# Expert down pieces of a two-layer decoder trunk: the output bank becomes the outermost loop

## The reference

```python
def swiglu(h, w_gate, w_up, w_down):
    return (jax.nn.silu(h @ w_gate) * (h @ w_up)) @ w_down

def moe_swiglu(h, w_router, w_gate, w_up, w_down):
    ...
    for e in range(N_EXPERTS):
        out = out + comb[..., e:e + 1].astype(h.dtype) * swiglu(h, w_gate[e], w_up[e], w_down[e])
    return out
```

## Time and profile before

| what | value |
|---|---|
| median of 3 runs | 1414.81 us (1414.27 to 1415.77) |
| the profiled execution's own time | 1414.73 us |
| its span, first to last instruction | 1412.9 us |
| TensorE busy with matmuls | 1391.1 us, 10414 matmuls |
| VectorE busy / ScalarE busy | 1141.0 us / 920.1 us |
| HBM over the span | 312 GB/s |
| mean granted TensorE clock | 0.997 of full speed |
| stretch of the experts' matmuls | about 445 us to 1400 us |

### The profile page before, as it was taken

How to read it: one execution, slowest core, us unless ns; L and a number is a source line. 1 busy time by engine, 2 the same in 40 slices (tenths; PEclk the granted TensorE clock), 3 DMA queues, 4 the chain that set the end, 5 groups by cost and what they waited for, 6 DMA issues and landing times.

```text
span 1412.9 us, 24835 instructions
## 1 busy us (share of the span) xinstructions
PE 1391.1 (98%) x10414; PEld 1263.2 (89%) x10416; DVE 1141.0 (81%) x1042; ACT 920.1 (65%) x901; POOL 61.1 (4%) x72
## 2 busy tenths in 40 slices
PE   9999999999999999999999999999999999999996
PEld 7899999998888988888888888888888888888884
DVE  6676555558756999888988888888898898888886
ACT  3845444444445777777777777777777777777764
POOL 2030000003001200000000000000000000000030
PEclk9999999999999999999999999999999999999998
DMA  8456765554217999999999999999999999999951
GB/s 344 149 209 231 249 230 187 202 184 145 96 55 314 419 407 415 379 393 366 377 378 393 372 377 393 367 379 387 361 382 377 398 367 379 390 375 370 376 200 47
DMA packets 63582, 438.64 MB, mean 310 GB/s; under 512 B 7550, under 2 KB 7678, under 8 KB 12272
## 3 DMA queue, kind: packets, MB, share of 16 engines
q1 hardware_dynamic: 58752, 422.60, 78.5%
q10 hardware_dynamic: 3568, 10.57, 2.2%
q0 software_dynamic: 1152, 3.88, 0.8%
HBM read 431.44 MB, written 9.04 MB: 312 GB/s over the span
## 4 chain that ended last, share of the span: by engine, by line
PE 96%; POOL 2%; DVE 1%; ACT 1%; issue 0%; DMA 0%; DVEq 0%; POOLq 0%; ACTq 0%
PE ps L1909 43%; PE ps L1934 22%; PE ps L1602 11%; PE ps L1625 5%; PE ps L1513 3%; PE ps L1664 2%; PE ps L1767 2%; PE ps L1545 2%; PE ps L1916 1%; POOL hn L1449 1%; POOL hn L1452 1%; PE ps L1711 1%; PE ps L1739 1%; PE ps L1503 0%; PE ps L1897 0%
## 5 line engine op out<-in xcount | busy, mean ns | idle before, releaser
L1275 DVE TENSOR_TENSOR w_lo<-ring,w_hi 128x2048 fp32r<-128x2048 f32 x336 | 766.9, 2291 | 101.0 <-ACT w_hi L676 100.2
L676 ACT CAST w_hi<-ring 128x2048 fp32r<-128x2048 f32 x336 | 640.9, 1911 | 147.1 <-PE ps L1909 147.0
L1909 PE MATMUL ps<-w_hi,xg_hi 128*96 128x256 f32 x1792 | 248.0, 281 | 1.2 <-DVE xg_lo L1281 1.2
L1909 PE MATMUL ps<-w_lo,xg_hi 128*96 128x256 f32 x1792 | 239.9, 276 | 0.0
L1909 PE MATMUL ps<-w_hi,xg_lo 128*96 128x256 f32 x1792 | 239.9, 276 | 0.0
L1909 PEld LDWEIGHTS ps<-w_hi,xg_lo 128*96 128x96 f32 x1792 | 214.1, 161 | 0.0
L1909 PEld LDWEIGHTS ps<-w_lo,xg_hi 128*96 128x96 f32 x1792 | 214.1, 161 | 0.0
L1909 PEld LDWEIGHTS ps<-w_hi,xg_hi 128*96 128x96 f32 x1792 | 212.7, 161 | 1.3 <-DVE xg_lo L1281 1.3
L872 DVE TENSOR_TENSOR w_lo<-ring,w_hi 128x2048 fp32r<-128x2048 f32 x56 | 130.1, 2325 | 73.8 <-ACT w_hi L489 73.7
L489 ACT CAST w_hi<-ring 128x2048 fp32r<-128x2048 f32 x56 | 106.7, 1907 | 98.3 <-PE ps L1602 87.4
L1934 PE MATMUL ps<-w_lo,ht_hi 128*96 128x512 f32 x448 | 124.2, 398 | 0.2 <-DVE w_lo L1275 0.2
(11 more groups left out here) (288 smaller groups left out, 1239.1 us busy)
## 6 DMA issues: line engine op xcount, KB each, us to landing
ring<-in_moe_w_gate SPq DMA_DIRECT2D x112, 1024.0 KB, 7.2
ring<-in_moe_w_up SPq DMA_DIRECT2D x112, 1024.0 KB, 7.1
ring<-in_moe_w_down SPq DMA_DIRECT2D x112, 1024.0 KB, 7.2
ring<-in_ffn_w_gate SPq DMA_DIRECT2D x14, 1024.0 KB, 4.9
ring<-in_ffn_w_up SPq DMA_DIRECT2D x14, 1024.0 KB, 4.9
ring<-in_ffn_w_down SPq DMA_DIRECT2D x14, 1024.0 KB, 5.0
ring<-in_lru_w_in SPq DMA_DIRECT2D x7, 1024.0 KB, 13.8
ring<-in_attn_w_qkv SPq DMA_DIRECT2D x6, 1024.0 KB, 4.8
```

What stands on the lines that cost most here:

```text
L676: nc.scalar.copy(w_hi[:, (SPLITS + n) % PARTS], ring[:, s]).then_inc(hi_done, 1)
L1275: V.tensor_tensor(w_lo[:, part], ring[:, ORDER_MOE[n % SLOTS]], w_hi[:, part].bitcast(F32), ALU.subtract).then_inc(lo_done, 1)
L1909: mm = nc.tensor.matmul(ps[0:CAP, c % 2, m * CHF:(m + 1) * CHF], xs[a][:, k], w[b][:, k], start=(k == 0 and (a, b) == (0, 0)), stop=(k == ...
```

## The change

In `down`, the loop over the output half g becomes the outermost one. Each down piece now runs all three passes (six matmuls) into bank 2 and then all three passes into bank 3. The wait `low_part` stands ahead of the third pass of either half, so it is issued twice in a piece, first after four matmuls where it was after eight. The count of matmuls and weight loads, their shapes and their operands stay the same. `parts_used` is still increased by the last matmul of the piece. With `halves`, `y_low_done` is increased by the sixth matmul of the piece, where it was the tenth.

```diff
-                for a, b in PASSES:
-                    if b:
-                        low_part(i, n)
-                    by_half = halves and b
-                    for f, g in [(f, g) for g in range(2) for f in range(2)] if by_half else [(f, g) for f in range(2) for g in range(2)]:
-                        mm = nc.tensor.matmul(ps[0:CAP, 2 + g, :], hs[a][:, c % 2, f], w[b][:, f, g * 512:(g + 1) * 512],
-                                              start=(c == 0 and f == 0 and (a, b) == (0, 0)),
-                                              stop=(c == NCH - 1 and f == 1 and b == 1))
-                        if by_half and (f, g) == (1, 0):
-                            mm.then_inc(y_low_done, 1)
+                for g in range(2):
+                    for a, b in PASSES:
+                        if b:
+                            low_part(i, n)
+                        for f in range(2):
+                            mm = nc.tensor.matmul(ps[0:CAP, 2 + g, :], hs[a][:, c % 2, f], w[b][:, f, g * 512:(g + 1) * 512],
+                                                  start=(c == 0 and f == 0 and (a, b) == (0, 0)),
+                                                  stop=(c == NCH - 1 and f == 1 and b == 1))
+                    if halves and g == 0:
+                        mm.then_inc(y_low_done, 1)
                 mm.then_inc(parts_used, 1)
```

## The result

The changed kernel takes 1427.95 us (median of 4 runs, 1426.13 to 1428.84) against 1415.08 us (1414.27 to 1415.77) for the kernel before on the same chip: a ratio of 1.0086, with an interval of 1.0071 to 1.0100. It is slower by 12.9 us. The forecast was 1415.2 us, between 1409.5 and 1421.0.

A forecast was written before the change was run, and what follows sets the result against it. TensorE's unbroken matmul stream was taken as the bound. The profiled 1414.73 us plus pace 0, waits 0 and end +0.42 gave 1415.15, and with the runs' median 0.08 higher 1415.2 us; range 1409.5 to 1421.0.

The forecast's parts named there:

- What bounds the kernel: Whole span: TensorE busy 98%; between about 445 and 1390 us, time is the pace of one unbroken matmul stream.
- the signs that I had named as fatal: Down piece of 2.76 us or less, or 2.84 or more, or a step over 8.46 us, would make the prediction wrong.
- zero for the pace: Down pieces: the new order leaves the 0.2333 us per matmul unchanged, so the 1344 matmuls add 0 us.
- the low bound of -8.7: Down pieces: 1344 matmuls at twice the 256-column pace, 0.2268 us each instead of 0.2333, would save 8.7 us.
- my third rival: Gate and up behind down pieces fall into the slow pace, 0.1166 us a matmul: +32 us, 1447 us; chance 0.08.
- It decides from 9 steps on: Gate and up: the slow pace, at 0.31 us a step, would decide the outcome once 9 steps took it.
- The faster one: Down pieces: the 512-wide matmul pace falls to 0.2268 us, giving 1406.5 us, or 1410.8 for half; chance 0.16.
- The slower one, by banks: Down pieces: six matmuls in a row into one bank raise the pace to 0.2375 us, +5.6, 1420.8 us; chance 0.11.
- The wait for the low part: Mid-stream down pieces: the low weights arrive at least 0.40 us early, so the earlier, doubled wait costs 0, at most +1.1 us.
- That rival: Mid-stream down pieces: the low part comes late; seven pieces losing half a us each give +3.5, 1418.7 us; chance 0.03.
- The end: Last two down pieces: TensorE idles for the late low part, and the end moves by +0.42 us, bounds 0 and +0.93.

The follow-up runs named there:

- the two bank runs: Kernel before with each piece's first six matmuls in bank 2, last six in bank 3: 1415.91 us; changed kernel with banks 2 and 3 alternating: 1425.86 us.
- the run with the banks alternating: Changed kernel with its operand order and both waits kept, matmuls alternating between banks 2 and 3, except in the last piece: 1425.86 us, ratio 1.0078.
- the kernel that is faster than before: Kernel before with passes one and two of each down piece ordered by bank, third pass left as it was: 1413.73 us, ratio 0.9983.
- loads of after alone: Kernel before with only the loaded activations in the change's order, except in the last piece; streamed weights and banks as before: 1423.62 us, ratio 1.0042.

## Why the prediction was wrong

**What bounds the kernel** was right: TensorE's unbroken stream, and the pace is what everything hung on. Two of the signs that I had named as fatal are there: a piece of 2.76 us, and a step of 8.55, over 8.46.

**The step that failed** is the one in which I took zero for the pace. I argued from the earlier trace rows that order doesn't matter, but those are 256-wide matmuls and show the pace of the piece that is reordered; I asked only what the new order does to its own 12 matmuls. What the earlier trace rows hinted at, gaps 0.01 us shorter in the bank-ordered pass, is real for the whole piece: 2.80 to 2.76 us, times 110 = -4.4 us, inside the low bound of -8.7. What I didn't carry into the sum is that the order also sets the pace of the 48 matmuls behind the piece. It was my third rival, with a chance of 0.08, and it is what happened: 85 more groups at the slow pace, 85 x 0.154 = +13.1 us.

**The rival's own size was off.** I wrote a step of 96 gate and up matmuls; it has 48 (24 of gate and 24 of up, 5376 in all over 112 steps). With the right count its full price is 105 x 0.154 = +16 us and not +32, and 1431 us would have been the end of the range to weigh, not 1447. "It decides from 9 steps on" should have been 18. The range left it out either way. The evidence against it, that the piece begins and ends with the same shapes and count, wasn't evidence: the trace before had shown two paces with the same shapes. Since the paces were seen to depend on what came ahead of them, and the change alters exactly what comes ahead of every gate-and-up group, 0.08 was too little.

**The rivals on the 512-wide pace.** The faster one came true by half, 2.80 to 2.76 us a piece, -4.4 of its -8.7 us, and was outweighed; it comes from the order of the loads, not from the banks. The slower one, by banks, falls: the two bank runs show nothing in either direction. The sentence of the Trainium skill against the change (Perfetto Trace Analysis, Matmul Optimizations, use all 8 banks) gives the right sign for a reason that the bank runs don't bear out: six matmuls in a row into one bank cost nothing here.

**The wait for the low part** was right in the stream: L1934 has no wait for `w_lo` there, and one wait more in a piece costs nothing, 1.0005 with an interval that holds 1. That rival falls.

**The end** was right in its steps: the wait is 1.17 us, forecast as about 1.3 (the difference of 1394.0 and 1395.28); bank 2's copy starts before the piece is over, and the scatter has no wait for ScalarE. Its size was not: I had +0.42 us. Where the clock held, in the run with the banks alternating, the end is 25.5 us long against 25.2 to 25.4 in four kernels with the old end, about 0.1 to 0.3 more. With the clock down it is 27.1, +1.7, and of this 0.7 to 0.8 us is the new order, by the 26.3 to 26.4 us of the old order with the clock down. I had not priced a fall of the clock in either kernel. That the longer wait brings it about is not shown.

**The start** of the experts, +2.6 us in the profiled execution, has nothing to do with the new order: the instructions are the same up to there, and the kernels with and without the change show it both ways (438 to 440 us at 1.00 with the end alone changed, at 0.50 in the kernel that is faster than before). It belongs to the execution, and of the 12.9 us between the two profiles only 10.3 are in stretches that the change touches. All four runs of the changed kernel have a mean granted clock of 0.993 or 0.995. Like compared with like, the order costs less than the medians say: at 0.998 the runs of the kernel before take 1413.9 to 1415.0 us, and those of the two kernels with the changed order of loads (banks alternating, loads of after alone) 1423.2 to 1423.8, about 9 us more. That alone lies outside the range.

**What stays open.** Shown is that the sequence of loaded activations, and not the banks, the streamed weights or the waits, sets the length of the piece and, but for a few groups, how many groups behind it are slow. The place of the transposes has a part in it too. Which property of the sequence does it isn't settled. It isn't the number of immediate repeats (twelve repeats give the shortest piece and 67 slow groups), nor the last four loads (the same four give 1 slow group and 109). Reversing the two halves alters the piece, so which half comes first counts; their place in memory is one way to explain it, and not shown apart. That the reads of the loads and TensorE's queue fall into one of two rhythms is a picture, not a finding.

## What to carry to other kernels

Where TensorE's stream is the bound, the pace of a matmul is not a constant of its shape: look in the trace for two paces of the same instruction, and if there are two, expect any reordering ahead of it to move matmuls from one to the other. Measure a reordering by the distance from one step to the next and not by the part that was reordered; here that part became 1.4% shorter while the kernel became 0.9% slower. A separate run for each thing that a loop order changes at once (bank, streamed operand, loaded operand, waits) is cheap and settled here what no reading of the old trace could. When the old trace shows two paces, price the slow one by counting the matmuls behind one reordered piece, and let it into the range.

## What was not expected of the hardware

- The same 256-column fp32r matmuls, each with its own load of 96 columns, run at 0.1134 or at 0.1167 us each, for 48 in a row and across steps, at the full granted clock. Nothing in the trace waits in either case.
- 512-column matmuls with these operands take 0.229 to 0.233 us each, depending on which halves are loaded in which order. The order of the streamed operand, the PSUM bank and satisfied waits make no difference to this (2.800 and 2.760 us a piece with either).
- One wait of 2.0 us on TensorE, behind hundreds of us of unbroken matmuls, was followed by the 1.2 GHz level, within about 1 us of the wait's end, in seven of twelve traces; with a second wait of 1.15 us or more behind it, the clock fell at that one in four of five. The 512-wide matmuls then took 0.43 us each.
